# Which slots of an eight-row gather ring TensorE and VectorE take in a value turn

## What is computed

```python
def peer_ffn(hn, wq, subkeys, u, v):          # 8 heads, 128 keys a side, 16 experts a head
    ...
        top, sel = lax.top_k(cand, PEER_TOPK)
        expert = jnp.take_along_axis(cidx, sel, axis=-1)
        g = jax.nn.softmax(top, axis=-1)
        act = jax.nn.gelu(jnp.einsum('cd,chkd->chk', xc, u[expert]).astype(jnp.float32))
        return jnp.einsum('chk,chkd->cd', (g * act).astype(v.dtype), v[expert])
```

## Time and profile before

| | us |
|---|---|
| median of 3 executions | 2530.28 (2526.9 to 2530.45) |
| the profiled execution, its own time | 2534.32 |
| its span in the profile | 2532.5 |
| busy: TensorE matmul, VectorE, GpSimd, ScalarE | 1613.9, 1408.7, 1301.8, 401.5 |
| granted TensorE clock, mean, as a share of full speed | 0.802 |
| first and last prompt gather issued | 726.0, 2476.8 |

### The profile page before, as it was taken

The page is one execution under the profiler, slowest core; times in us unless marked ns, Lnnn a source line. Parts: engine busy times, 40 slices in busy tenths (PEclk is TensorE's granted clock), DMA queues, the critical chain, the costliest instruction groups (busy, mean ns, idle before and its releaser), DMA issues.

```text
span 2532.5 us, 17694 instructions
## 1 busy us (share of the span) xinstructions
PE 1613.9 (64%) x5401; PEld 791.3 (31%) x5401; DVE 1408.7 (56%) x3543; ACT 401.5 (16%) x1075; POOL 1301.8 (51%) x1080
## 2 busy tenths in 40 slices
PE   5999988798935936853656466756444535353454
PEld 2334865445522313331213223413211212111121
DVE  2200047511158655568656765577666777888753
ACT  2000335413211310201011121010110000001010
POOL 0000000000237677567557666667678788877883
PEclk9999968897976966867878777788867777777777
DMA  6111500332248889888989898899999999998996
GB/s 203 67 67 68 167 1 1 137 107 83 67 164 290 310 284 323 317 290 291 367 301 352 320 338 314 330 367 350 377 345 338 350 339 323 338 323 320 325 333 218
DMA packets 194805, 646.09 MB, mean 255 GB/s; under 512 B 30664, under 2 KB 38056, under 8 KB 193848
## 3 DMA queue, kind: packets, MB, share of 16 engines
q0 software_dynamic: 152896, 562.11, 61.6%
q1 hardware_dynamic: 41816, 82.86, 9.6%
HBM read 638.78 MB, written 10.29 MB: 256 GB/s over the span
## 4 chain that ended last, share of the span: by engine, by line
PE 34%; POOL 32%; issue 11%; DMA 11%; DVE 7%; ACT 3%; SPq 1%; POOLq 0%; DVEq 0%; ACTq 0%
POOL arena L724 32%; PE bank L786 9%; PE bank L1310 6%; DMA arena<-in_peer_v,expert 5%; DVE arena L2233 3%; DMA arena<-in_peer_u,expert 3%; PE bank L986 3%; PE bank L1071 2%; PE bank L1176 1%; PE bank L1210 1%; PE bank L1103 1%; PE bank L808 1%; PE bank L1003 1%; PE bank L1052 1%; POOL arena L713 1%
## 5 line engine op out<-in xcount | busy, mean ns | idle before, releaser
L1310 PE MATMUL bank<-arena 128*128 128x512 f32 x1280 | 716.2, 713 | 665.7 <-DMA arena<-in_peer_v,expert 349.1
L724 POOL DMA_INDIRECT arena<-in_peer_v,expert x512 | 660.7, 1291 | 195.4 <-issue 146.6
L724 POOL DMA_INDIRECT arena<-in_peer_u,expert x512 | 584.4, 1141 | 330.5 <-issue 146.4
L2233 DVE CUSTOM_DVE_ANT_0 arena<-arena 128x1024 f32<-128x1024 f32 x512 | 618.3, 1215 | 234.6 <-DMA arena<-in_peer_u,expert 233.9
L1310 PEld LDWEIGHTS bank<-arena 128*128 128x128 f32 x1280 | 276.7, 228 | 1094.1 <-issue 566.9
L2249 DVE SCALAR_TENSOR_TENSOR arena<-arena 128x1024 f32<-128x1024 f32 x192 | 246.4, 1283 | 276.5 <-DMA arena<-in_peer_v,expert 244.9
L786 PE MATMUL bank<-arena 128*128 128x512 f32 (+3 forms) x560 | 227.0, 566 | 0.0
L713 POOL DMA_INDIRECT arena<-in_cache_slc_k,row_idx x16 | 15.9, 993 | 377.5 <-PE bank L1052 372.9
L1521 ACT ACTIVATE arena<-arena 128x16 f32<-128x16 f32 x32 | 6.9, 215 | 812.3 <-DVE arena L2233 812.3
L786 PEld LDWEIGHTS bank<-arena 128*128 128x128 f32 (+1 forms) x560 | 94.0, 170 | 132.4 <-issue 127.5
L1660 ACT ACTIVATE arena<-arena 128x128 f32<-128x128 f32 x320 | 99.7, 388 | 220.6 <-DVE arena L2224 220.5
(11 more groups left out here) (292 smaller groups left out, 1905.2 us busy)
## 6 DMA issues: line engine op xcount, KB each, us to landing
arena<-in_w_in SPq DMA_DIRECT2D x6, 2048.0 KB, 7.8
arena<-in_w_out SPq DMA_DIRECT2D x2, 4096.0 KB, 19.2
arena<-in_peer_u,expert POOLq DMA_INDIRECT x512, 6.2
arena<-in_peer_v,expert POOLq DMA_INDIRECT x512, 6.1
arena<-in_w_mq SPq DMA_DIRECT2D x2, 2048.0 KB, 9.4
arena<-in_peer_wq SPq DMA_DIRECT2D x2, 2048.0 KB, 10.6
arena<-in_w_mo SPq DMA_DIRECT2D x2, 2048.0 KB, 14.3
arena<-in_cache_mem_k SPq DMA_DIRECT2D x2, 2048.0 KB, 14.4
```

The costliest lines, as they stand in the source:

```text
L724: pool.indirect_dma_start(out=ring[:, k, :], out_offset=None, in_=a[name][0], in_offset=bass.IndirectOffsetOnAxis(ap=idx, axis=0)).then_in ...
L1310: ins = pe.matmul(banks[6 + half][:, :], diag[:, nth % 2, j, :], ring[:, k, half * 512:(half + 1) * 512], start=(first and j == 0), stop=( ...
L2233: dve.tensor_tensor_reduce(out=ring[:, k, :], in0=ring[:, k, :], in1=hn3[:, t, :], scale=1.0, scalar=0.0, op0=ALU.mult, op1=ALU.add, accum ...
```

## The change

One constant. TensorE takes slots 0 to 4 of each v turn; `V_SLOTS`, computed from it, becomes 5, 6, 7 in place of 1, 3, 6. All the rest of the program's text is the same.

```diff
@@ -58,7 +58,7 @@
 RING = 8
 TURNS = SLOTS // RING
 ROWS = 2 * SLOTS
-PE_SLOTS = (0, 2, 4, 5, 7)
+PE_SLOTS = (0, 1, 2, 3, 4)
 CMP_UNITS = [(0, 0), (0, 1), (1, 0), (1, 1), (0, 2), (1, 2)]
```

## The result

The changed kernel takes 2576.5 us (median of 4; 2573.3 to 2579.3), the kernel before 2528.6 in the same comparison: a ratio of 1.019, 95% interval 1.017 to 1.021, so 48 us slower. The forecast was +22, to 2552, in a range of 2522 to 2588.

A forecast was written before the change was run, and what follows sets the result against it. GpSimd's gather calls, with TensorE's slots having no room, were taken to bound the kernel; 14 x 1.4 + 7 x 0.3 + 10 x 0.4 + 1.5 - 3 = +24 us, cut to +22, gave 2552 us, range 2522 to 2588.

The forecast's parts named there:

- What bounds the kernel: GpSimd's gather calls lead the chain; TensorE's slots have no room, and no backlog swallows a delay of POOL.
- the signs named beforehand: POOL's TensorE waits rise from 35 to over 60; refills trail TensorE's rows by 0.8 us; TensorE's busy time, clock stay.
- The absorbed rival: DMA and POOL's queue are the true limit, so POOL's delay only shortens landing time: 2530 to 2534; chance 0.13.
- (a): Each head's second value turn (x=1): TensorE's rows free slots later, holding POOL's refills; +1.2 us a turn, bounds 0 and 1.9.
- 0.7 us won back: In x=1 turns, later gather calls miss VectorE operations that lengthened them; 0.7 us taken of up to 1.0.
- (b): Each head's first value turn (x=0): VectorE's rows at slots 5 to 7 end 0.9 us late; +0.2 a turn on average.
- (c): TensorE's slots in x=0 turns: its fifth row comes late for slot 4 in a few turns; +1.5 us in all.
- (d): TensorE ends x=0 turns earlier and starts other work sooner, which helps in 3 cases: -3 us.
- The count: Of 31 x=1 turns, 14 pay 1.4 us, 7 pay 0.3, 10 pay 0.4; total +24 cut to +22 for easing.
- Fewer meetings of VectorE and POOL: Rival: VectorE's rows in a row meet and lengthen fewer gather calls: 2513 us; chance 0.12.
- The clock: Rival: five contiguous TensorE rows in x=0 turns keep the clock up into the x=1 burst: net 2525; chance 0.03.
- Slower still: Rival: in the last third VectorE, POOL and TensorE form one loop, so (a) and (b) add fully: 2575 to 2600; chance 0.10.

The follow-up runs named there:

- held_x1: Kernel before, slots unchanged, with GpSimd's calls for slots 0 to 4 behind x=1 turns also waiting for TensorE's five rows: 2580.7 us, ratio 1.019.
- x1_only: Changed slots (TensorE 0 to 4, VectorE 5 to 7) in x=1 value turns alone, against the kernel before: 2562.0 us, ratio 1.013.
- x0_v456: Kernel before with, in x=0 turns alone, VectorE's rows at slots 4 to 6, TensorE's at 0 to 3 and 7: 2538.7 us, ratio 1.005.
- x0_only: Changed slots (TensorE 0 to 4, VectorE 5 to 7) in x=0 value turns alone, against the kernel before: 2539.0 us, ratio 1.0045.
- held_x0: Kernel before, slots unchanged, with GpSimd's calls for slots 0 to 4 behind x=0 turns also waiting for TensorE's five rows: 2572.2 us, ratio 1.018.
- mirror: Kernel before with VectorE's rows at slots 0 to 2 and TensorE's at 3 to 7 in all value turns: 2521.4 us, ratio 0.999.

## Why the prediction was right and wrong

*What bounds the kernel*: right. POOL's calls were the chain, TensorE's slots had no room, and the delay went into the time. held_x1 shows it with the hold alone. Of the signs named beforehand, TensorE's unchanged busy time and clock failed (1613.9 to 1590.1 us, 0.802 to 0.783), and the lag behind its rows is 0.27 us from the second on; the others came.

*The absorbed rival*: wrong, as held. DMA drops to 0.61 during a hold, and x1_only loses 34 us.

*(a), the x=1 turns, mis-sized.* I had 22.9 us for them (14 x 1.2 + 7 x 0.3 + 10 x 0.4); x1_only measured 34. The gross delay was near: slot 7's refill comes 1.6 us later behind TensorE's start (median of the x=1 turns, 14.75 to 16.32 us; 1.9 worked out for slot 5). Two smaller points cancelled in the example: later rows free their slots with a lag of 0.27 us, not 0.78, and the second row took 2.75 us in place of 2.15. The first refill was also less tight than I wrote: its idle time of 0.37 us is only 0.07 over the plain 0.30. What failed is the **0.7 us won back**. I let the later calls miss VectorE's operations. They met others: VectorE's rows 5 to 7 and its next u rows follow one another there at about 2 us. The example above has calls of 1.57 and 1.24 us from the fifth on, and the mean u call is 0.10 us longer, 512 x 0.10 = 51 us. The v calls give 0.10 back, and the sum of the lengthening over 0.94 us is 283 us before and 284 after. In x1_only all calls together are 3.5 us shorter and POOL's idle time is 33 us longer. Without the 0.7 my sum would have been 14 x 1.9 + 7 x 0.3 + 10 x 0.4 = 32.7 us. That this comes so near is in part luck, for its count was wrong too: not 14 turns pay and 17 hardly, but 26 of 30 have a held refill, and 24 of the 29 stretches from one x=1 burst to the next are longer in x1_only, by 1.2 us on average over all.

*(b), VectorE late in x=0 turns.* The mechanism occurs as worked out, at 1.3 us in place of 0.9 (7.5 against 6.2 us from call to start):

```profile
2212.35 1.28 DVE L2249 SCALAR_TENSOR_TENSOR arena<-arena 128x1024 f32<-128x1024 f32 x1
2213.71 1.22 DVE L2233 CUSTOM_DVE_ANT_0 arena<-arena 128x1024 f32<-128x1024 f32 x1
```

The u row starts right behind VectorE's last value row, with no idle time, where it had 2.26 us. x0_v456, without this lateness, is as slow as x0_only; I find no price for it.

*(c) and (d), TensorE in x=0 turns, mis-sized*: +1.5 and -3 on paper, and with (b) at 14 x 0.2 some +1 for these turns; x0_only measured +11. What failed is that (c) worked out TensorE's fifth row alone. Beyond the plain 0.30 a call, POOL's waits at slots 1 to 3 behind x=0 turns, for TensorE's second to fourth row, rise from 4 to 19 us in x0_only, and those at slot 4 only from 3 to 5 (sums over the timelines). So the holds that I had in the x=1 turns alone are in 18 of the 31 x=0 turns too. For the early end of TensorE's turns, the 3 us of gain, no run shows anything.

*The count*, which the forecast cut from 24 to 22 for turns that ease each other: the two halves give 34 + 11 = 45 and the change 48. No easing between x=0 and x=1 turns shows, though the intervals, some 14 us to either side for x1_only, are too wide to show 2 us.

*Fewer meetings of VectorE and POOL* fell: the calls' sum is unchanged. *The clock* fell too: the mean granted clock went from 0.802 to 0.783, and from 0.74 to 0.69 in 2040 to 2360 us, and the idle time ahead of the x=1 burst grew (15.6 us in the earlier trace rows, 18.5 us above; medians of 11.9 and 14.2 us); its first row still takes 3.75 us. By the rule of the Trainium skill that the prediction cites for this rival (TensorE: Matmul & The Clock Gate, "HAM oscillation") grouping should have kept the clock up; here the gap between the groups grew and the clock fell. *Slower still* was nearer than the forecast: its start was 2575, though not by (b), as it had it.

## What to carry to other kernels

In a ring whose slots are refilled in order by one engine, give the first slot to the engine that ends its first row first, and check the time between two frees against the time between two refills (1.72 against 1.24 us here): a slow engine's rows belong apart and late in the turn. Ask of a delay not only whether something hides it, but whether the engine that is delayed can run faster afterwards; time lost by an engine without a backlog stays lost. And work out every row of a turn, not only the last, in each kind of turn, before you decide which turns pay.

## What the runs showed of the hardware

A gather call that meets one of VectorE's 1024-column float32 operations ends 0.80 to 0.85 us behind the operation's end: 490 of the 501 prompt gather calls over 1.0 us of the kernel before do. The sum of this lengthening over 0.94 us stayed within 267 to 295 us in all thirteen kernels, wherever the slots lay. The number of VectorE's operations is the same in all of them, so whether the sum follows it isn't shown.

A held gather call starts 0.27 us (median) behind the end of the TensorE row that frees its slot, and 0.78 us where the wait that holds it stands in the trace as an instruction of its own ahead of the call: for slot 0 of the u turns wherever TensorE has that slot, and for the added waits of held_x1 and held_x0. The length of the row makes no difference: slot 0 of the kernel before starts 0.78 us behind first rows of 1.95 us as behind those of 3.75, and slot 3 of mirror 0.27 us behind all 11 first rows that held it, of which seven took 3.48 to 3.78 us.

In the 471 bursts of the thirteen kernels that began after TensorE had been idle for over 10 us, the first value row took 3.36 to 3.78 us, in most of them 3.75 to 3.78; rows later in such a burst take 1.88. In the two windows of 4 us shown for the kernel before and for the changed one, the granted clock is 0.50 in the first and 1.00 and 0.82 in the second.
